# A hybrid decoder layer: split per-head keys for the attention scores, head outputs through memory, first scores in the last scan

## What is computed

```python
def reference(x, mem, w_in, ...):                       # x (1, 1024, 1024)
    h = x @ w_in[l]                                     # 14 groups of columns
    ...
    o_a = _gated_delta_rule(qa, ka, va, g, beta)        # 4 heads of 128: a scan over chunks
    o_a = _rmsnorm_f32(o_a, dn_norm_w[l]) * silu(z_a)
    q_abs = einsum('bshd,hrd->bshr', q_s, w_uk[l])      # queries taken into the latent space, rank 128
    c = _rmsnorm_f32(ckv, kv_norm_w[l])                 # latent keys and values, 1024 x 128
    lat = _dsa_attention(q_abs, c, q_i, k_i, w_i, slopes)
    #   per block of 128 queries: scores of an indexer, the best 256 keys of each query,
    #   s = einsum('bqhr,bqkr->bqhk', qa, c_sel) * 64 ** -0.5 - slopes * dist ; softmax ; times c_sel
    o_s = einsum('bshr,hrd->bshd', lat, w_uv[l]) * silu(z_s)
    ...                                                 # o_m: attention into 256 memory tokens
    y = concatenate([o_a, o_s, o_m]) @ w_out[l]
    return layernorm(alpha * x + y)
```

## Time and profile before

| | |
|---|---|
| median of 3 runs | 865.08 us (862.08 to 866.42) |
| the profiled execution, its time and span | 863.28 us, 861.5 us |
| TensorE busy | 764.0 us, 89% |
| VectorE, ScalarE, GpSimd busy | 494.5, 462.0, 145.3 us |
| share of the chain that ended last | TensorE 62%, VectorE 19%, ScalarE 11% |
| granted TensorE clock, mean | 0.955 |
| DMA | 60.87 MB, 71 GB/s on average |

### The profile page before, as it was taken

One profiled execution on the slowest core, in us unless ns is written; L12 is line 12 of the kernel. 1 busy time (PEld: TensorE's weight loads), 2 busy tenths in 40 slices (PEclk: granted clock), 3 DMA queues, 4 the chain that ended last, 5 costly groups with the idle time before them and its releaser, 6 DMA issues.

```text
span 861.5 us, 11407 instructions
## 1 busy us (share of the span) xinstructions
PE 764.0 (89%) x3996; PEld 620.6 (72%) x3996; DVE 494.5 (57%) x1068; ACT 462.0 (54%) x1045; POOL 145.3 (17%) x248
## 2 busy tenths in 40 slices
PE   6999969899987999699996999895698998998975
PEld 5888857778876888578895788773476676774764
DVE  5634869756664475544655378763556556536532
ACT  4523566888768875788677852224443334323300
POOL 0000000053021510242101520001002033212330
PEclk9999989999998999899997999997989999999988
DMA  9312110124001320014000241008401122111201
GB/s 357 100 49 75 49 37 26 37 65 141 25 26 49 96 86 25 21 60 127 25 25 25 88 131 49 25 25 266 148 1 49 37 86 86 49 50 61 74 25 49
DMA packets 56424, 60.87 MB, mean 71 GB/s; under 512 B 16048, under 2 KB 42928, under 8 KB 55984
## 3 DMA queue, kind: packets, MB, share of 16 engines
q1 hardware_dynamic: 56368, 60.15, 21.3%
HBM read 45.46 MB, written 14.68 MB: 70 GB/s over the span
## 4 chain that ended last, share of the span: by engine, by line
PE 62%; DVE 19%; ACT 11%; issue 6%; DMA 1%; SPq 0%; POOL 0%; DVEq 0%; ACTq 0%; POOLq 0%
PE bank L846 15%; PE bank L854 9%; PE bank L856 9%; PE bank L855 9%; PE bank L860 3%; ACT cst L1658 3%; PE bank L1090 2%; PE bank L1118 2%; PE bank L1010 2%; DVE score L1280 2%; PE bank L1025 2%; PE bank L997 2%; PE bank L1023 2%; DVE mix_lo L1525 1%; DVE arena L1489 1%
## 5 line engine op out<-in xcount | busy, mean ns | idle before, releaser
L854 PE MATMUL bank<-x_hi,ring_split 128*128 128x512 f32 x480 | 200.9, 419 | 7.4 <-DVE x_lo L1225 7.3
L855 PE MATMUL bank<-x_lo,ring_split 128*128 128x512 f32 x480 | 191.6, 399 | 0.0
L856 PE MATMUL bank<-x_hi,ring_split 128*128 128x512 f32 x480 | 191.6, 399 | 0.0
L1658 ACT ACTIVATE cst<-score,sel 128x1024 bf16<-128x1024 f32 (+2 forms) x192 | 166.9, 873 | 29.0 <-DVE sel L1302 27.6
L854 PEld LDWEIGHTS bank<-x_hi,ring_split 128*128 128x128 f32 x480 | 93.2, 194 | 23.4 <-DVE ring_split L1233 7.2
L856 PEld LDWEIGHTS bank<-x_hi,ring_split 128*128 128x128 f32 x480 | 92.8, 193 | 20.8
L855 PEld LDWEIGHTS bank<-x_lo,ring_split 128*128 128x128 f32 x480 | 93.2, 194 | 15.6
L1759 ACT ACTIVATE arena<-arena,misc 128x512 f32<-128x512 f32 (+7 forms) x32 | 24.8, 775 | 81.0 <-DVE misc L1495 81.0
L1575 ACT ACTIVATE arena<-bank 128x512 f32<-128x512 f32 (+1 forms) x108 | 49.8, 499 | 34.3 <-PE bank L860 9.7
L846 PE MATMUL bank<-w_out_hi,mix_hi 128*128 128x512 f32 x128 | 56.0, 438 | 6.7 <-DVE mix_lo L1525 4.2
L1545 DVE SCALAR_TENSOR_TENSOR arena<-qkvT,bank 128x512 f32<-128x512 f32 x16 | 11.0, 688 | 80.0 <-PE bank L846 80.0
(11 more groups left out here) (247 smaller groups left out, 1438.9 us busy)
## 6 DMA issues: line engine op xcount, KB each, us to landing
ring<-in_w_groups SPq DMA_DIRECT2D x30, 512.0 KB, 3.5
x_raw<-in_x_t SPq DMA_DIRECT2D x8, 512.0 KB, 9.3
side_z<-stage SPq DMA_DIRECT2D x16, 256.0 KB, 2.1
w_out_sb<-in_wout_t SPq DMA_DIRECT2D x2, 2048.0 KB, 13.0
zgT<-side_z SPq DMA_DIRECT2D x8, 512.0 KB, 3.9
qkvT<-in_x SPq DMA_DIRECT2D x8, 512.0 KB, 4.7
out_y<-arena SPq DMA_DIRECT2D x8, 512.0 KB, 2.8
ring<-in_wmem_t SPq DMA_DIRECT2D x2, 1024.0 KB, 4.7
```

The source lines that it names most:

```text
L854: nc.tensor.matmul(dst, hi, xh, start=(c == 0), stop=False)
L855: nc.tensor.matmul(dst, hi, xl, start=False, stop=False)
L856: last = nc.tensor.matmul(dst, lo, xh, start=False, stop=(c == KT - 1))
L1658: sc.activation(signs[order[e] % 2][:, 0:w], score[:, score_at(b):score_at(b + 1)], ACT.Sign, scale=-1.0, bias=candidate[:, b - 2:b - 1], ...
```

## The change

- **Scores from per-head keys.** Four new steps `kh`, inside the scan of the last head, multiply the latent keys with `w_uk` once for all blocks (plain float32, 64 columns for each of two heads). ScalarE writes the rounded result of a head into rows 0 to 63 of its `key_stack`, VectorE the rest (what the rounding left) into rows 64 to 127. `qabs` is gone. `qsplit` takes its place: a block's raw queries are loaded twice, into rows 0 to 63 and 64 to 127, ScalarE rounds them into `q_hi`, VectorE puts the rest into `q_lo`. A score tile is now two split matmuls, `q_hi` and `q_lo` against the stack.
- **Head outputs kept in memory.** `oall` (all heads) becomes `o_head` (one head). After a head's scan SyncE stores it to `side_o`, and each block's outputs are loaded into `mix`, where GpSimd scales them in place.
- **First scores inside the last scan.** The last three steps of the last scan carry block 3's scores, and no side projection; these are spread over the steps before. `cT` moves into the inversion. Scores wait for their own block's selection alone.
- SyncE: the latent weights `wuk`, `wuv` come at the start, and of `consts` 512 columns fewer are loaded; block 3's queries come inside the scan; the output weights are issued before the gates and without waiting for the last stores. The first matmul of a `scanV` no longer waits for the scaled keys `nw`.

The core of the diff:

```diff
+            if not more and s < NLEV - 1:
+                steps += [("cT", s - LEV0)]
...
-            steps += [("scanV", h, b), 1.2, ("scanS", h, b), 1]
+            if more or b < N_LAST_FILLED:
+                if not more:
+                    steps += [[("q_first",)], [("kh", 0, 0)], [("kh", 0, 1)], [("kh", 1, 0)], [("kh", 1, 1), ("qsplit", first_block)]][b]
+                steps += [("scanV", h, b), 1.2, ("scanS", h, b), 1]
+            else:
+                n = b - N_LAST_FILLED
+                steps += [("scanV", h, b), *scores(first_block, n), ("scanS", h, b), *(scores(first_block, 3) if b == NB - 1 else [])]
...
-    for e in [("cT", 0), ("cT", 1), ("deltanet_scale", first), ("qabs", first), *[t for h in range(SAH) for t in scores(first, h)], ("msc", first, 0), ("msc", first, 1)]:
+    for e in [("msc", first_block, 0), ("msc", first_block, 1), ("deltanet_scale", first_block)]:
...
-            queues.append((0.5, [[("qabs", nb)], scores(nb, 0), *[scores(nb, h) for h in range(1, SAH)]]))
+            queues.append((0.5, [[("qsplit", nb)], scores(nb, 0), *[scores(nb, h) for h in range(1, SAH)]]))
...
+            def store_outputs(h):
+                sp.wait_ge(*released(("O", h, NB - 1)))
+                sp.dma_start(side_o[:, :, h * DND:(h + 1) * DND].rearrange("b p d -> p b d"), o_head).then_inc(o_stored, 16)
+
+            def load_queries(n):
+                cols = slice(BLOCK_ORDER[n] * P, (BLOCK_ORDER[n] + 1) * P)
+                for i in range(2):
+                    to = q_raw(n)[64 * i:64 * i + 64, :].rearrange("p (h t) -> p h t", h=SAH)
+                    sp.dma_start(to, side_q[0:2, :, cols].rearrange("m (o d) t -> d (m o) t", o=2)).then_inc(queries_back[query_buffer(n)], 16)
+                sp.dma_start(q_mem(n), side_q[2:4, :, cols].rearrange("m p t -> p m t")).then_inc(mem_queries_back[query_buffer(n)], 16)
...
+                if e[0] == "scanS" and e[2] == NB - 1 and e[1] < DNH - 1:
+                    store_outputs(e[1])
+                if e == ("q_first",):
+
+                    sp.wait_ge(*filled(("XY", DNH - 1, 0, NLEV - 1)))
+                    sp.wait_ge(side_stored, 16 * (1 + max(n for e_, n in staged_at.items() if e_[0] == "side" and e_[1] < 4)))
+                    load_queries(0)
...
-            sp.wait_ge(*filled(last_use[groups[-1]]))
-            sp.wait_ge(side_stored, 16 * len(staged))
...
-            sp.dma_start(wukT, wuk_t).then_inc(side_mem_back, 16)
-            load_queries(0)
-            sp.dma_start(wuv.rearrange("p (h d) -> p h d", h=SAH), w_uv.rearrange("a h r d -> r (a h) d")).then_inc(side_mem_back, 16)
+            def load_outputs(n):
+                sp.dma_start(mix[:, 0:DNW], side_o[BLOCK_ORDER[n]]).then_inc(o_back, 16)
+
+            sp.wait_ge(*filled(last_use[groups[-1]]))
             sp.dma_start(kmT[:, :], side_mem[0]).then_inc(side_mem_back, 16)
+            load_queries(1)
             sp.dma_start(vm[:, :], side_mem[1]).then_inc(side_mem_back, 16)
-            load_queries(1)
             for i in range(2):
                 half = slice(i * 512, (i + 1) * 512)
                 sp.dma_start(wout[:, :, half], wout_t[:, :, half]).then_inc(w_sem[i], 16)
+            sp.wait_ge(side_stored, 16 * len(staged))
+            for i in range(2):
                 load_gates(i)
+            store_outputs(DNH - 1)
+            sp.wait_ge(o_stored, 16 * DNH)
+            load_outputs(0)
...
+                if n:
+
+                    sp.wait_ge(*filled(("mixT", BLOCK_ORDER[n - 1], 0)))
+                    load_outputs(n)
...
+                elif k == "kh":
+                    m, t = e[1:]
+                    pe.wait_ge(latent_weights_loaded, 32)
+                    pe.wait_ge(*released(("cT", t)))
+                    if not first(e):
+                        pe.wait_ge(*vacated(e))
+                    nc.tensor.matmul(ps(e)[:, :], wuk[:, m * P:(m + 1) * P], c_half[t], start=True, stop=True).then_inc(fill_of(e), 1)
...
-                    nc.tensor.matmul(ps(e)[:, 0:hi - lo], qab[:, h * P:(h + 1) * P], cT[:, lo:hi], start=True, stop=True).then_inc(fill_of(e), 1)
+                    keys = keys_of(h)[:, lo:hi]
+                    group(ps(e)[:, 0:hi - lo], [(q_hi[:, h * P:(h + 1) * P], keys), (q_lo(PLACE[b])[:, h * P:(h + 1) * P], keys)]).then_inc(fill_of(e), 1)
...
+                elif k == "kh":
+                    m, t = e[1:]
+                    dve.wait_ge(head_keys_hi_ready, order[e])
+                    for odd in range(2):
+                        h = 2 * m + odd
+                        keys = keys_of(h)[:, t * 512:(t + 1) * 512]
+                        last = v.scalar_tensor_tensor(keys[64:128, :], ps(e)[64 * odd:64 * odd + 64, :], key_scale(h), keys[0:64, :].bitcast(F32),
+                                                      ALU.mult, ALU.subtract)
+                    last.then_inc(release_of(e), 1)
+                elif k == "qsplit":
+                    n = PLACE[e[1]]
+                    dve.wait_ge(head_queries_hi_ready, n + 1)
+                    v.tensor_tensor(q_lo(n), q_raw(n), q_hi[:, :].bitcast(F32), ALU.subtract).then_inc(head_queries_split, 1)
...
-                    if (b, h, c) == (BLOCK_ORDER[0], 0, 0):
-
-                        dve.wait_ge(keys_selected, N_SEL)
+                    if (h, c) == (0, 0) and b >= 2:
+
+                        dve.wait_ge(keys_selected, SELECT_ORDER.index(b) + 1)
...
+                elif k == "kh":
+                    m, t = e[1:]
+                    act.wait_ge(*filled(e))
+                    if m == 1:
+
+                        act.wait_ge(conv_done, 6 * DNH)
+                    for odd in range(2):
+                        h = 2 * m + odd
+                        last = copy(keys_of(h)[0:64, t * 512:(t + 1) * 512], ps(e)[64 * odd:64 * odd + 64, :], key_scale(h))
+                    last.then_inc(head_keys_hi_ready, 1)
+                elif k == "qsplit":
+                    n = PLACE[e[1]]
+                    act.wait_ge(*queries_loaded(n))
+                    if n:
+
+                        before = BLOCK_ORDER[n - 1]
+                        act.wait_ge(*filled(("sc", before, SAH - 1, len(idx_chunks(before)) - 1)))
+                    copy(q_hi[:, :], q_raw(n)).then_inc(head_queries_hi_ready, 1)
...
-                    if PLACE[b]:
-
-                        pool.wait_ge(*filled(("mixT", BLOCK_ORDER[PLACE[b] - 1], 0)))
+                    pool.wait_ge(o_back, 16 * (PLACE[b] + 1))
                     m = mix[:, 0:512].rearrange("p (h d) -> p h d", h=4)
-                    g.tensor_tensor(m, oall[:, b, :, :], s_orn[:, 4 * b:4 * b + 4].unsqueeze(2).broadcast_to([P, 4, P]), ALU.mult).then_inc(deltanet_scaled, 1)
+                    g.tensor_tensor(m, m, s_orn[:, 4 * b:4 * b + 4].unsqueeze(2).broadcast_to([P, 4, P]), ALU.mult).then_inc(deltanet_scaled, 1)
```

140 lines of the change are left out of this document (81 added, 59 removed), and 2 rows, old and new, of the table POOL_OF.

## The result

The changed kernel takes **868.1 us** (median of 8 runs, 866.97 to 869.99) against 864.09 before (8 runs, 862.08 to 866.42). The ratio is 1.0056, with a 95% interval of 1.0043 to 1.0069: slower by 4 us, where 849 was forecast with a range of 836 to 858. The profiled execution took 868.49 us, with a span of 866.7 (before: 861.5). Two disturbed executions are left out of all medians of this document: one of 1488.62 us (scores_after) and one of 912.02 us (the kernel before, beside no_affine, scores_after, kh_late and pool_late).

A forecast was written before the change was run, and what follows sets the result against it. TensorE (busy 764.0 of 861.5 us) was taken to bound the kernel, VectorE the last scan's first half. Against 863.3: -6.6 (scan and gap) -0.5 (blocks 3, 4) -10.1 (attention) +2.5 (clock) = -14.7, 848.6; forecast 849, range 836 to 858.

The forecast's parts named there:

- first scan step no longer waits (heads 0 to 2): Scans: the first matmul no longer waits for the scaled weights, whose copy was done; priced at nothing.
- up to step 0 of the last head: Ahead of the last scan: more side projections and key transposes move its first copy 4 us, from 549.82 to 553.8.
- steps 0 to 4: Last head's scan: eight key subtractions (5.5 us) and one of queries (0.69) on full VectorE add 6.2 us.
- step 4 to the first exponential of block 4: Scan's end and gap: step 4's copy at 580.7, later steps 2.4 us each, block 4's first exponential at 600.8.
- blocks 3 and 4: First two attention blocks: pace kept, 0.5 us less for the latent queries that TensorE no longer makes.
- five blocks: scores, latent queries, clock: Later attention blocks: 10.1 us less for halved score pieces and dropped latent queries, 2.5 us more for the clock.
- The attention blocks: Part pricing block transitions: 2.2, 2.2 and 3.5 us gained in three, 1.1 in each of two others, 10.1 together.
- the first rival: One gain fails: key steps serial on VectorE (four times 2.0 us), or boundaries are VectorE's; 856 us, chance 0.20.
- the upper value of 2.5 us: Block boundaries: longer TensorE waits lower its clock, up to 1.25 us at each of two boundaries, 2.5 us lost.
- The slower rival: Clock falls in the scan's tail, first block's projections and boundaries: twenty us more work at 1.2 GHz, 868; chance 0.07.
- The scan: Last head's scan: ScalarE copies (4.8 us) and key matmuls (3.4 us) lie in idle time; VectorE's additions cost 6.2 us.
- Edits at nothing: Edits priced at zero: head outputs through memory (scale at about 674), query DMAs, constants, dropped scan wait, own selection waits.

The follow-up runs named there:

- scores_after: The changed kernel with the first block's scores put back behind the last scan, side projections spread over all eight steps again: 873.82 us, ratio 1.0106.
- no_affine: The changed kernel without GpSimd's two 1024-wide row operations (gains, offsets) in all blocks but the last, so not computing the layer: 856.95 us, ratio 0.9922.
- kh_late: The changed kernel with old scan wait, query split one block earlier, and VectorE's part of each key tile behind its scan copy: 856.17 us, ratio 0.9909.
- pool_late: The changed kernel with old scan wait, earlier query split, GpSimd's row operations after VectorE's mixed-row split, and maximum with scaling as one operation: 849.07 us, ratio 0.9830.
- after_pool_late: The changed kernel with one wait added: GpSimd's row operations wait for VectorE's split of the mixed rows; nothing left out: 857.91 us, ratio 0.9921.
- before_pool_late: The kernel before with GpSimd's row operations waiting for VectorE's mixed-row split, and the one-column maximum and its scaling as one operation: 854.25 us, ratio 0.9881.
- nw_back: The changed kernel with the wait for the negated weights back ahead of the first scan matmul of each half of a head: 866.77 us, ratio 1.0040.
- combined: pool_late plus the edit of kh_late, VectorE's key subtractions behind its scan copies: 847.1 us, ratio 0.9801 to the kernel before.

## Why the prediction was wrong

Its sum was -14.7 us against the profiled execution; the spans differ by +5.2. By its own terms:

| term | forecast | measured |
|---|---|---|
| first scan step no longer waits (heads 0 to 2) | 0 | +3.7 |
| up to step 0 of the last head | +4.0 | +3.4 |
| steps 0 to 4 | +6.2 | +9.9 |
| step 4 to the first exponential of block 4 | -16.8 | -15.2 |
| blocks 3 and 4 | -0.5 | -0.8 |
| five blocks: scores, latent queries, clock | -7.6 | +3.3 |
| the last block and the end | 0 | +1.0 |

(measured: differences of the landmarks, 501.74 - 498.08 for the first, then the intervals between the rows of the table above. The last 1.0 us lies behind block 7's `o` step, 31.9 to 32.9 us; no run was made on it.)

**The step that failed** is in "The attention blocks": "the new query copy and subtraction, 0.6 and 0.7, take most of the time they leave". The 0.7 came from a subtraction in the earlier trace rows that reads a bank. The new one reads two tensors from on-chip memory and was placed where GpSimd works on the rows of an earlier block. Five of seven took 2.82 us, each 2.13 more, 10.7 together, and the next scores wait for them. after_pool_late and no_affine, which take away nothing of VectorE's own work, give back 10.2 and 11.2. The rows to see it were in the trace of the kernel before, groups by line and shape:

```profile
L1525 DVE TENSOR_TENSOR mix_lo<-arena,mix_hi 128x1024 fp32r<-128x1024 f32 x8 | 15.9, 1986 | 1.8 <-ACT mix_hi L1575 1.8
...
L1494 DVE TENSOR_TENSOR misc<-misc 128x1 f32<-128x1 f32 x16 | 7.6, 476 | 0.6
```

The first has a mean of 1.99 us where its shortest takes 1.22, the second 0.48 for one column, where 0.16 is usual. A stalled operation counts as busy, so no idle time gave it away. The same two in the changed kernel:

```profile
L1623 DVE TENSOR_TENSOR mix_lo<-arena,mix_hi 128x1024 fp32r<-128x1024 f32 x8 | 11.0, 1379 | 2.0 <-ACT mix_hi L1673 2.0
...
L1592 DVE TENSOR_TENSOR misc<-misc 128x1 f32<-128x1 f32 x16 | 3.1, 194 | 0.6
```

So the change did not bring the stall, it moved it. Counted as time above each operation's shortest, VectorE loses 6.1 us (mixed rows) and 5.1 (maxima) in the kernel before, 11.2 in all. In the changed kernel it is 1.3, 0.5 and 10.7 for the queries, 12.5 in all. But now the block's first scores wait for the stalled operation. What that costs is read from the five blocks: without the stall they are 8.7 us shorter in the kernel before (145.2 to 136.5, before_pool_late) and 16.7 in the changed one (148.5 in nw_back to 131.8 in pool_late, the earlier query split included; both have the maximum as one operation). Of the 10.9 us by which the forecast missed these blocks, 8.0 are this difference, with what it does to the clock, and 2.9 are the next point.

The Trainium skill has the rule (SBUF — State Buffer, Who interferes with whom): an instruction of VectorE with two inputs in on-chip memory contends with a GpSimd instruction that reads it, whoever issues first has the shared ports for the whole instruction, and the other blocks fully. The runs agree in all three points: 2.82 against 0.69 us, 0.21 for the form with a scalar operand, and 2.02 against 1.04 for GpSimd when it came second. It was not weighed in the prediction.

**The second part of that step** was to count what TensorE saves at a boundary, 10.1 us. With the stall away from both kernels, before_pool_late takes 136.5 us from the o step of block 4 to that of block 0 (658.62 to 795.11) and pool_late 131.8 (656.14 to 787.90). So, with the clock at 1.00 in both, split scores and dropped latent queries are worth 4.7 us there, not 10.1 (7.6 with the clock's 2.5): the pieces of the earlier trace rows stood between VectorE's reductions, and halving them in part made TensorE wait longer (for reductions 3.9 us in four waits in before_pool_late, 7.3 in six in pool_late). Nor do the rows give the 10.1: halved, with the 0.35, the pieces shown make 1.1 us at 670.48 and 3.1 at 784.33 and 794.79, where the prediction has 2.2 and 3.5. The 4.93 us of 5 in the earlier trace rows, its sign that the boundary is VectorE's, was itself the stall in part: a maximum of 2.04 us from 779.57 and a mixed-row subtraction of 1.96 from 781.71. That was half of the first rival, and the prediction gave it 0.20 together with the scan.

**The clock**: the upper value of 2.5 us had the right sign. The grants were 0.94, 0.94, 0.89, 1.00 and 0.94, where the kernel before had 0.94 in the last block alone. after_pool_late has 0.94 in one of the five and pool_late 1.00 in all, so the falls went with the stalled subtraction. The slower rival's 868 is the measured time by luck, not by its mechanism: the last scan steps ran at 1.00 (570 to 600), and the stretch of the first block's two projections at the grants of the kernel before (0.80 in 623 to 640 and 0.91 in 640 to 659 in both). The grant of 0.70 in 600 to 623 (0.93 before) did not cost what the rival says: blocks 3 and 4 together came 0.8 us faster.

**"The first scan matmul no longer waits ... their copy was done"** was wrong. The earlier trace rows begin at 585, and the wait is in the scans of heads 0 to 2: 6.8 us at 261.34 in the kernel before. Taking it away was no gain but a loss. Price in medians: 1.3 (not clear of noise), 2.9 and 3.6 us in three pairs of kernels.

**The scan**: "the eight ScalarE copies and the four key matmuls lie in the idle time of their engines" is true of those engines, but VectorE waited for their end, 1.2 to 1.6 us in three of the four steps, 3.7 us more than the forecast in all. That is 0.9 a step, under half of the 2.0 that the first rival had for it. Steps 5 to 7 came at 2.2, 2.7 and 2.6 us (forecast 2.4). The last reduction ended 10.9 us after step 4's copy (forecast 8.8), at 598.4, and from there to the exponential of block 4 were 10.8 us (forecast 11.3). So this term was 1.6 us short of a forecast gain of 16.8, and the sign of it is what scores_after confirms.

**Edits at nothing** that held: GpSimd's scale of the head outputs started at 674.8 (forecast about 674) and nobody on the path waited for it; the output weights were there at the exponential. The extra table load took 1.28 us, as the other did.

**The sum of it**: repaired (old wait, earlier query split, VectorE's keys behind its copy) and with the stall out of both, the change is worth 7.2 us (847.1 against 854.25), about half of what was forecast. The 21.0 us from the changed kernel to combined are, one edit after the other, 8.2 for the split out of GpSimd's way, 2.9 for the scan step's wait, 7.9 for GpSimd's rows and the maximum, and 2.0 for the keys, which is not clear of noise. The kernel before gains 9.8 us from the two edits of the third step.

## What to carry to other kernels

Before adding or moving an operation of VectorE with two inputs in on-chip memory, look at what GpSimd does at that moment, and take its price from a row of the same operand kinds; a group whose mean is far above its shortest may already be stalled, and a stall that stands somewhere harmless can be moved to where others wait for it. Where GpSimd's work has slack, one wait that holds it back can pay: it gave 10 us in both kernels (in the one before together with the maximum in one operation). A wait that only stands ahead of filler work may be what keeps the filler for the time when it is needed; before taking it away, see what the engine has left behind it.
